# A gated delta rule kernel: the products of the state ahead of the coupling products, and the loads of the triangular solve shared by two DMA queues

## The chip, the cores and the metric

The kernel runs on one core of a Trainium2 chip. The metric is the device time of one launch in microseconds (us), from three runs. The engines are PE (matrix products), DVE and ACT (vector work), POOL (here memsets and DMA issues) and SP (DMA issues only). SP and POOL each own a DMA queue; both queues feed the same 16 DMA engines.

## The reference, cut to what matters

One layer for 2048 prompt tokens and 8 x 8 sample tokens. Half of it is windowed attention in three head groups with different strides; the other half, to which most of the change belongs, is the gated delta rule on 6 heads of width 128:

```python
lower = jnp.where(strict, jnp.einsum('...ik,...jk->...ij', kb, kc) * dmask, 0.0)
...
sol = lax.linalg.triangular_solve(jnp.eye(C) + lower, rhs, left_side=True, lower=True)
...
def step(S, xs):
    v_new = u_i - w_i @ S
    o = (q_i * jnp.exp(G_i)[..., None]) @ S + a_i @ v_new
    S = S * jnp.exp(g_last) + (k_i * jnp.exp(g_last - G_i)).T @ v_new
```

Every step needs the state S of the step before. The triangular systems do not depend on S.

## The kernel before, in words

The program is a row of blocks with a barrier between them: modulate, project (to about 1600 us of the trace), attend_prompt (to about 1800), attend_samples, delta_prompt (about 1862 to 2246), delta_samples and the tail with the output projections. The change is in attend_prompt and delta_prompt.

**delta_prompt** handles 16 chunks of 128 tokens in 8 pairs p. It is a software pipeline over the iteration `it` from -2 to 7: `grams` and `mask` build the systems of pair it+2 (tile UA), `solve` inverts the 32 x 32 diagonal blocks of a pair, `couple32`, `close32`, `couple64` and `close64` join these blocks into the inverse of the whole chunk (tile TT), and `of_state`, `solved` and `outputs` step the state S through chunks c = 2 it and c+1. The order on each engine is the order of the calls in the loop over ITS; engines meet at semaphores only.

The solve of all 96 blocks of a pair (2 chunks x 6 heads x 4 blocks) is one elimination on DVE, 31 pivots of two instructions in eight pieces. A block lies in it in one partition, which no engine can lay out, so the data goes through DRAM: `system(p)` on SP stores UA to u_d, waits for the store (u_out), and reads the diagonal blocks into sub_u with 8 DMAs of 384 runs of 128 bytes; `solution(p)` stores the result sub_w to w_d, waits (sub_out), and reads it into the diagonal of TT with 8 DMAs of 192 runs of 128 bytes. On DVE `turn_diag` waits for TT and makes the transposed blocks T, which `couple32` reads on PE; `gates` prepares decays for the pair after, `residual`, `state` and `result` are the DVE's part of the state's step. The step of a chunk goes kS (of_state) on PE, `residual` (rv) on DVE, Tr (solved) on PE, `new_values` (vn) on ACT, kv (outputs) on PE, `state` (S) on DVE. POOL issues only the store of each chunk's result (`store`).

In iteration `it` DVE runs residual(c), pieces 3 and 4 of the solve of pair it+1, state(c), pieces 5 to 7, mask(a), result(c), mask(a+1), residual(c+1), gates, turn_diag of pair it+1, state(c+1), pieces 0 and 1 of the solve of pair it+2, result(c+1), piece 2.

**attend_prompt** handles 3 groups of 16 blocks. DVE copies each block's result into the tile rows, SP stores it. The tile is one for all groups, so DVE waits at the start of groups 1 and 2 (`enter`) until the rows of the group before are stored. At the start of group 2 SP also begins the loads for attend_samples into space that groups 0 and 1 have left: five small ones, then the key cache kc in 8 parts. POOL scales q_s into q_bd_s when the five small ones are in.

## Time and profile before

| | us |
|---|---|
| median of 3 runs | 2910.11 |
| lowest, highest | 2894.85, 2912.45 |
| the profiled execution | 2896.57 |
| its span | 2894.9 |
| busy in the span: PE, DVE, ACT, POOL | 2608.3, 1083.4, 776.8, 153.3 |
| mean granted TensorE clock | 0.936 |

The profiled execution is one more run, with the time of the fast end of the three. The span is counted from the first to the last instruction; 1.7 us lie around it. Times of rows are microseconds from the start of the span.

### The profile page before, as it was taken

The numbers are of one execution on the slowest core, as the hardware profiler recorded it, in microseconds if no ns is written. First come the engines' busy times: TensorE is split into PE (matmuls) and PEld (weight loads), VectorE is DVE, ScalarE is ACT, GpSimd is POOL, SyncE is SP. The second block draws the span as 40 slices with busy tenths as digits, with TensorE's granted clock in tenths as the row PEclk, the third lists the DMA queues.
The fourth block names the chain that finished last, engine by engine and source line by source line (L and its number), as shares of the span: only waits on it lengthen the run. The fifth ranks groups of instructions, "written<-read, shape, count | busy, mean of one in ns | idle before, by whom it ended". The sixth has DMA issues, their size and how long they took to land. (4 is left out here: it accounts for less than half of the span.)

```text
span 2894.9 us, 41003 instructions
## 1 busy us (share of the span) xinstructions
PE 2608.3 (90%) x16430; PEld 2384.2 (82%) x16430; DVE 1083.4 (37%) x2593; ACT 776.8 (27%) x1677; POOL 153.3 (5%) x289
## 2 busy tenths in 40 slices
PE   6799999999999999999999798658777749999997
PEld 1799999999999999999999677347767539999775
DVE  3344444300000000000021465357775557675554
ACT  2222222211111111111100455234444123232343
POOL 0000000000000000000011000000000001111000
PEclk9899999999999999999999899768888669999998
DMA  7111112221111121111121715666443065555442
GB/s 282 61 70 69 69 69 77 82 75 67 67 67 67 67 83 72 67 67 67 68 79 46 303 36 201 210 140 159 111 107 109 29 216 162 179 177 191 146 141 75
DMA packets 249382, 320.42 MB, mean 111 GB/s; under 512 B 69874, under 2 KB 202242, under 8 KB 237348
## 3 DMA queue, kind: packets, MB, share of 16 engines
q1 hardware_dynamic: 201732, 201.46, 22.3%
q0 software_dynamic: 21136, 104.24, 9.5%
q10 hardware_dynamic: 26384, 12.98, 1.7%
q8 instruction: 82, 1.34, 0.2%
q14 instruction: 48, 0.39, 0.0%
HBM read 206.52 MB, written 112.11 MB: 110 GB/s over the span
## 5 line engine op out<-in xcount | busy, mean ns | idle before, releaser
L71 PE MATMUL ps_proj<-h_lo,w_hi 128*128 128x424 f32 (+1 forms) x2320 | 820.9, 354 | 26.1 <-DVE w_lo L401 26.1
L72 PE MATMUL ps_proj<-h_hi,w_lo 128*128 128x424 f32 (+1 forms) x2320 | 821.4, 354 | 0.0
L73 PE MATMUL ps_proj<-h_hi,w_hi 128*128 128x424 f32 (+1 forms) x2320 | 820.8, 354 | 0.0
L401 DVE TENSOR_TENSOR w_lo<-w_raw,w_hi 128x1024 fp32r<-128x1024 f32 x58 | 71.1, 1225 | 1080.7 <-ACT w_hi L320 1080.7
L71 PEld LDWEIGHTS ps_proj<-h_lo,w_hi 128*128 128x128 f32 x2320 | 436.3, 188 | 45.1 <-DVE w_lo L401 27.0
L72 PEld LDWEIGHTS ps_proj<-h_hi,w_lo 128*128 128x128 f32 x2320 | 436.0, 188 | 9.7
L73 PEld LDWEIGHTS ps_proj<-h_hi,w_hi 128*128 128x128 f32 x2320 | 436.1, 188 | 8.8
L358 ACT ACTIVATE stage<-ps_proj 128x424 f32<-128x424 f32 (+1 forms) x200 | 104.6, 524 | 755.8 <-PE ps_proj L73 755.8
L71 PE MATMUL ps_fm<-u_lo,w_tail_hi 128*128 128x256 f32 (+1 forms) x768 | 221.4, 288 | 11.6 <-DVE u_lo L2293 7.0
L72 PE MATMUL ps_fm<-u_hi,w_tail_lo 128*128 128x256 f32 (+1 forms) x768 | 219.6, 286 | 0.0
L73 PE MATMUL ps_fm<-u_hi,w_tail_hi 128*128 128x256 f32 (+1 forms) x768 | 219.4, 286 | 0.0
L71 PEld LDWEIGHTS ps_fm<-u_lo,w_tail_hi 128*128 128x128 f32 x768 | 146.2, 190 | 12.9 <-DVE u_lo L2293 7.6
L73 PEld LDWEIGHTS ps_fm<-u_hi,w_tail_hi 128*128 128x128 f32 x768 | 146.3, 190 | 0.0
L72 PEld LDWEIGHTS ps_fm<-u_hi,w_tail_lo 128*128 128x128 f32 x768 | 146.3, 190 | 0.0
L442 DVE SCALAR_TENSOR_TENSOR conv<-stage,side,conv 128x2048 f32<-128x2048 f32 x54 | 126.2, 2336 | 0.0
L71 PE MATMUL ps_out<-w_tail_lo,m_hi 128*128 128x512 f32 (+1 forms) x272 | 108.3, 398 | 0.3
L72 PE MATMUL ps_out<-w_tail_hi,m_lo 128*128 128x512 f32 (+1 forms) x272 | 107.5, 395 | 0.0
L73 PE MATMUL ps_out<-w_tail_hi,m_hi 128*128 128x512 f32 (+1 forms) x272 | 107.5, 395 | 0.0
L833 ACT ACTIVATE probs<-scores,neg 128x256 f32<-128x256 f32 (+1 forms) x192 | 86.2, 450 | 72.3 <-DVE neg L798 72.3
L368 ACT ACTIVATE conv<-conv 128x2112 f32<-128x2112 f32 x18 | 35.5, 1971 | 170.1 <-DVE conv L445 170.1
L1597 DVE TENSOR_TENSOR sub_prod<-sub_u,sub_w 96x126 f32<-96x126 f32 (+22 forms) x248 | 62.2, 251 | 42.8 <-DMA sub_u<-scratch_u_d 35.2
L1423 PE MATMUL ps_a<-xkq_first 128*128 128x256 f32 x96 | 31.2, 493 | 45.5 <-DVE UA L1584 32.0
(372 smaller groups left out, 3580.2 us busy)
## 6 DMA issues: line engine op xcount, KB each, us to landing
w_raw<-in_w_feat SPq DMA_DIRECT2D x58, 512.0 KB, 4.4
scratch_conv_d<-conv POOLq DMA_DIRECT2D x18, 1056.0 KB, 4.7
scratch_g_d<-stage POOLq DMA_DIRECT2D x16, 1056.0 KB, 4.5
gates<-scratch_g_d SPq DMA_DIRECT2D x56, 256.0 KB, 3.0
scratch_z_d<-stage POOLq DMA_DIRECT2D x12, 1056.0 KB, 4.5
ada_w<-in_w_ada SPq DMA_DIRECT2D x6, 2048.0 KB, 10.0
z_f<-scratch_z_d ACTq DMA_DIRECT2D x16, 768.0 KB, 5.0
kc<-in_k_cache SPq DMA_DIRECT2D x8, 1152.0 KB, 21.5
```

The lines of the kernel that those rows point to most:

```text
L71: pe.matmul(out, ah, bl, start=start, stop=False)
L72: pe.matmul(out, al, bh, start=False, stop=False)
L73: return pe.matmul(out, ah, bh, start=False, stop=stop)
L358: last = act.activation(stage[:, j, at:at + n], ps[:, c, 0:n], func)
L368: act.activation(conv[:, j, :], conv[:, j, :], ACT.Silu).then_inc(conv_silu, 1)
L401: dve.tensor_tensor(w_lo[:, j, 0:KT * P], w_raw[:, j, 0:KT * P], f32(w_hi[:, j, 0:KT * P]), ALU.subtract).then_inc(lo_done[j], 1)
L442: dve.scalar_tensor_tensor(out=conv[:, j, 0:SEQ], in0=stage[:, j, n:n + SEQ], scalar=w, in1=conv[:, j, 0:SEQ], op0=ALU.mult, op1=ALU.add). ...
L833: act.activation(probs[:, x.slot, p, h, 0:P * x.kb], scores[:, x.slot, p, h, 0:P * x.kb], ACT.Exp, bias=neg[:, x.slot, head:head + 1], acc ...
L1423: last = pe.matmul(A[bank_of(c, u)][:, 256 * (h % 2):256 * (h % 2 + 1)], x[:, h, 0, :], x[:, h, :, :].rearrange("p a n -> p (a n)"), start ...
L1597: dve.tensor_tensor(sub_prod[:, 0:n, 0:m], u[:, i:i + 1, i + 1:].broadcast_to([NSUB, n, m]), w[:, 0:n, i:i + 1].broadcast_to([NSUB, n, m]) ...
```

## The change

In delta_prompt the 8 loads of each system and of each solution are split: 4 are issued by SP as before, the other 4 by POOL, each half with a semaphore of its own, and DVE waits for both. On PE, `solved(c+1)` comes ahead of `couple32(b)` and `outputs(c+1)` ahead of `close32(b)`; on ACT, `new_values(c+1)` comes ahead of `keep32(b)`; on DVE, both `gates` come behind `state(c+1)`. In attend_prompt the rows of group 1 get a second home, the first part of the value tile of group 0, so that DVE waits only once, in group 2 for the rows of group 0. The key cache's last part lies over this home, so SP waits for the rows of group 1 before it, and the small loads (but for ident) come behind it.

```diff
@@ attend_prompt @@
-        rows = sb("rows", [P, NBLK, GW])
+        own_rows = sb("rows", [P, NBLK, GW])
+        rows = [own_rows, first["v"][:, 0], own_rows]
...
@@ SP, enter(g) for g == 2 @@
+                kc = lambda s: sp.dma_start(late["kc"][:, s], t["k_cache"][s]).then_inc(late["k_in"][s // HALF], 16)
                 sp.wait_ge(o_full, 2 * NBLK)
+                for s in range(NSEQ - 1):
+                    kc(s)
+                sp.dma_start(late["ident"][:, :], t["ident"]).then_inc(late["small_in"], 16)
+                sp.wait_ge(row_stored[1], 16 * NBLK)
+                kc(NSEQ - 1)
                 sp.dma_start(late["q_in"][:, :, :], t["q_d"][:, :, SEQ:].rearrange("a p n -> p a n")).then_inc(late["small_in"], 16)
...
-                sp.dma_start(late["ident"][:, :], t["ident"]).then_inc(late["small_in"], 16)
-                for s in range(NSEQ):
-                    sp.dma_start(late["kc"][:, s], t["k_cache"][s]).then_inc(late["k_in"][s // HALF], 16)
@@ DVE, attend_prompt @@
             def enter(g):
-                if g:
-                    dve.wait_ge(row_stored[g - 1], 16 * NBLK)
+                if g == 2:
+                    dve.wait_ge(row_stored[0], 16 * NBLK)
@@ delta_prompt @@
-        u_out, sub_in = sem("u_out"), [sem(f"sub_in{j}") for j in range(2)]
-        sub_out, tt_in = sem("sub_out"), [sem(f"tt_in{j}") for j in range(2)]
+        u_out, sub_in = sem("u_out"), [[sem(f"sub_in{s}{j}") for j in range(2)] for s in range(2)]
+        sub_out, tt_in = sem("sub_out"), [[sem(f"tt_in{s}{j}") for j in range(2)] for s in range(2)]
...
+        def load_solution(q, p, s):
+
+            q.wait_ge(sub_out, 16 * (p + 1))
+            q.wait_ge(zeroed, 1)
+            if p >= 2:
+                q.wait_ge(Tr, 4 * (p - 2) + 4)
+            w = t["w_d"][p].rearrange("(s a n) (c r) -> s a c n r", s=2, a=P // SUB, r=SUB)
+            for a in range(P // SUB):
+                dst = TT[p % 2].rearrange("p c h r -> p (c h) r")
+                q.dma_start(dst[SUB * a + s:SUB * (a + 1):2, :, SUB * a:SUB * (a + 1)], w[s, a]).then_inc(tt_in[s][p % 2], 16)
+
+        def load_system(q, p, s):
+
+            q.wait_ge(u_out, 32 * (p + 1))
+            if p >= 2:
+                q.wait_ge(sub_step, 2 * PIVOTS * (p - 1))
+            u = t["u_d"][p].rearrange("(a j) c h (b i) -> a b (c h) j i", j=SUB, i=SUB)
+            for a in range(P // SUB):
+                at = (NSUB // 2) * s + 2 * NHB * a
+                q.dma_start(sub_u[p % 2][at:at + 2 * NHB], u[a, a]).then_inc(sub_in[s][p % 2], 16)
...
@@ SP, solution(p) and system(p) @@
-                for s in range(2):
-                    for a in range(P // SUB):
-                        dst = TT[p % 2].rearrange("p c h r -> p (c h) r")
-                        sp.dma_start(dst[SUB * a + s:SUB * (a + 1):2, :, SUB * a:SUB * (a + 1)], w[s, a]).then_inc(tt_in[p % 2], 16)
+                load_solution(sp, p, 0)
...
-                for s in range(2):
-                    for a in range(P // SUB):
-                        at = (NSUB // 2) * s + 2 * NHB * a
-                        sp.dma_start(sub_u[p % 2][at:at + 2 * NHB], u[a, a]).then_inc(sub_in[p % 2], 16)
+                load_system(sp, p, 0)
@@ POOL @@
             for it in ITS:
+                if has(it + 1):
+                    load_solution(pool, it + 1, 1)
                 if has(it):
                     store(2 * it)
+                if has(it + 2):
+                    load_system(pool, it + 2, 1)
+                if has(it):
                     store(2 * it + 1)
@@ PE @@
                     turn_keys(b + 1)
-                    couple32(b)
                 if has(it):
                     solved(c + 1)
                 if has(it + 1):
+                    couple32(b)
                     turn_values(b + 1)
-                    close32(b)
                 if has(it):
                     outputs(c + 1)
                 if has(it + 1):
+                    close32(b)
                     couple64(b), couple32(b + 1)
@@ DVE @@
-                if has(it + 3):
-                    gates(a + 2), gates(a + 3)
                 if has(it + 1):
                     turn_diag(b), turn_diag(b + 1)
                 if has(it):
                     state(c + 1)
+                if has(it + 3):
+                    gates(a + 2), gates(a + 3)
@@ ACT @@
                     keys(b + 1)
-                    keep32(b)
                 if has(it):
                     new_values(c + 1)
                 if has(it + 1):
+                    keep32(b)
                     values(b + 1)
```

What stands on DVE in an iteration, from `residual(c+1)` to `state(c+1)`, before and after (rv is residual's tile, ET that of gates, S the state):

```order
L1619 SCALAR_TENSOR_TENSOR rv<-ps_c0,coef,bv1 128x128 x3
L1619 SCALAR_TENSOR_TENSOR rv<-ps_c1,coef,bv1 128x128 x3
L1574 TENSOR_TENSOR ET0<-G_in0,causal_T 128x768
L1574 TENSOR_TENSOR ET1<-G_in1,causal_T 128x768
L1609 STREAM_TRANSPOSE T0<-TT1 32x6x32 x3
L1609 STREAM_TRANSPOSE T1<-TT1 32x6x32 x3
L1628 SCALAR_TENSOR_TENSOR S<-S,coef,ps_c0 128x128 x3
L1628 SCALAR_TENSOR_TENSOR S<-S,coef,ps_c1 128x128 x3
```

```order
L1636 SCALAR_TENSOR_TENSOR rv<-ps_c0,coef,bv1 128x128 x3
L1636 SCALAR_TENSOR_TENSOR rv<-ps_c1,coef,bv1 128x128 x3
L1626 STREAM_TRANSPOSE T0<-TT1 32x6x32 x3
L1626 STREAM_TRANSPOSE T1<-TT1 32x6x32 x3
L1645 SCALAR_TENSOR_TENSOR S<-S,coef,ps_c0 128x128 x3
L1645 SCALAR_TENSOR_TENSOR S<-S,coef,ps_c1 128x128 x3
L1589 TENSOR_TENSOR ET0<-G_in0,causal_T 128x768
L1589 TENSOR_TENSOR ET1<-G_in1,causal_T 128x768
```

The two gates moved behind the update of the state. The transposes, which wait for the solution's load, stay ahead of it.

On PE, behind the turned keys of chunk c+1 (L1439, after L1454). Tr is L1522 (after L1537), couple32 L1465 and L1466 (after L1480 and L1481), and the turned values L1447. Before, the last two of the twelve products of couple32 and what follows; after, the last keys and what follows:

```order
L1465 MATMUL ps_a0<-T0,UA2 32x32
L1466 MATMUL ps_a1<-T0,UA2 32x32
L1522 MATMUL ps_c0<-rv,TT0 128x128 x3
L1522 MATMUL ps_c1<-rv,TT0 128x128 x3
L1447 MATMUL ps_a2<-ident_d,xv3 128x128 x3
L1447 MATMUL ps_a3<-ident_d,xv3 128x128 x3
```

```order
L1454 MATMUL ps_a2<-ident_d,xkq_first 128x128 x3
L1454 MATMUL ps_a3<-ident_d,xkq_first 128x128 x3
L1537 MATMUL ps_c0<-rv,TT0 128x128 x3
L1537 MATMUL ps_c1<-rv,TT0 128x128 x3
L1480 MATMUL ps_a0<-T0,UA2 32x32
L1481 MATMUL ps_a1<-T0,UA2 32x32
```

Tr now comes ahead of the twelve small products, which read the transposed solution T0. In the same way kv moved ahead of close32, and on ACT the copies to vn ahead of those to Y32.

On SP, from the load of a solution to the next gates' load, before and after:

```order
L1346 DMA TT0<-scratch_w_d 16x12x32 x8
L1351 DMA scratch_u_d<-UA2 128x6x128
L1351 DMA scratch_u_d<-UA3 128x6x128
L1359 DMA sub_u1<-scratch_u_d 12x32x32 x8
L1328 DMA G_in0<-scratch_G_rows 128x768
```

```order
L1317 DMA TT0<-scratch_w_d 16x12x32 x4
L1368 DMA scratch_u_d<-UA2 128x6x128
L1368 DMA scratch_u_d<-UA3 128x6x128
L1327 DMA sub_u1<-scratch_u_d 12x32x32 x4
L1353 DMA G_in0<-scratch_G_rows 128x768
```

Both loads are halved. The other halves stand on POOL, between the stores, which were all that POOL had in this block (L1405 is the store, L1327 the system's load, L1317 the solution's), here after:

```order
L1405 DMA scratch_o_d<-o_d0 128x768
L1327 DMA sub_u0<-scratch_u_d 12x32x32 x4
L1405 DMA scratch_o_d<-o_d1 128x768
L1317 DMA TT0<-scratch_w_d 16x12x32 x4
L1405 DMA scratch_o_d<-o_d0 128x768
```

## Rows read from the trace of the kernel before

**Rows 1.** Busy time of one period, and of four: x, instructions; last columns clock, DMA share, GB/s
```profile
2121.20:2162.30 41.10, 32.18 (x336) 29.30 (x336) 31.22 (x105) 19.85 (x66) 1.08 (x2) 0.87 0.33 82
sum 166.10, PE 130.92 PEld 119.46 DVE 124.98 ACT 79.39 POOL 4.32; mean PE 32.73 PEld 29.87 DVE 31.25 ACT 19.85 POOL 1.08
```

**Rows 2.** Waits in 1880 to 2260 us: total us, times, longest us
```profile
DVE S L1628 <- PE ps_c L1529: 36.2, 10, 5.3
DVE sub_prod L1597 <- DMA sub_u<-scratch_u_d: 35.2, 8, 12.6
```

**Rows 3.** Timeline of SP: start us, duration us, line, DMA issues
```profile
1996.23 0.34 SPq L1337 DMA_DIRECT2D scratch_w_d<-sub_w  x1
1998.35 5.17 SPq L1346 DMA_DIRECT2D TT<-scratch_w_d  x8
2003.56 1.19 SPq L1351 DMA_DIRECT2D scratch_u_d<-UA  x2
2007.94 3.63 SPq L1359 DMA_DIRECT2D sub_u<-scratch_u_d  x8
2011.61 0.89 SPq L1328 DMA_DIRECT2D G_in<-scratch_G_rows  x2
```

**Rows 4.** Instructions by tile, sub_w: the store of the solution, ns min/median/max, first and last start
```profile
L1337 SPq DMA_DIRECT2D scratch_w_d<-sub_w x8: 320/338/343, 1912.5 to 2204.6; - x8
```

**Rows 5.** Timeline of DVE, same period, columns as in rows 3
```profile
2001.13 1.64 DVE L1619 SCALAR_TENSOR_TENSOR rv<-ps_c,coef,bv 128x128 f32<-128x128 f32 x6
2002.69 1.82 DVE L1574 TENSOR_TENSOR ET<-G_in,causal_T 128x768 f32<-128x768 f32 x2
2005.08 2.29 DVE L1609 STREAM_TRANSPOSE T<-TT 32x192 f32<-32x192 f32 x6 [0.57 <-DMA TT<-scratch_w_d]
2012.34 1.64 DVE L1628 SCALAR_TENSOR_TENSOR S<-S,coef,ps_c 128x128 f32<-128x128 f32 x6 [4.97 <-PE ps_c L1529]
2016.70 0.19 DVE L1597 TENSOR_TENSOR sub_prod<-sub_u,sub_w 96x31 f32<-96x31 f32 x1 [2.73 <-DMA sub_u<-scratch_u_d]
...
2024.03 1.63 DVE L1619 SCALAR_TENSOR_TENSOR rv<-ps_c,coef,bv 128x128 f32<-128x128 f32 x6
```

**Rows 6.** Timeline of PE, same period
```profile
2002.94 0.82 PE L1439 MATMUL ps_a<-ident_d,xkq 128*128 128x128 f32 x6
...
2006.76 2.91 PE L1522 MATMUL ps_c<-rv,TT 128*128 128x128 f32 x12
...
2011.37 1.60 PE L1529 MATMUL ps_c<-vn,k_dec 128*128 128x128 f32 x12
...
2020.57 2.93 PE L1507 MATMUL ps_c<-S,xkq 128*128 128x128 f32 x12
```

**Rows 7.** Timeline of ACT, same period
```profile
2003.98 1.69 ACT L1684 ACTIVATE k_dec<-ps_a,coef 128x128 f32<-128x128 f32 x6
...
2008.42 0.49 ACT L1746 ACTIVATE vn<-ps_c 128x384 f32<-128x384 f32 x1 [0.89 <-PE ps_c L1522]
```

**Rows 8.** Groups of instructions of POOL over the span: busy us, mean ns
```profile
L510 POOL DMA_DIRECT2D out_v_out<-v_rows x51 | 27.6, 542 | 121.2 <-DVE v_rows L425 117.6 <-issue 3.7
...
L493 POOL DMA_DIRECT2D scratch_norm_d<-norm_rows x12 | 6.0, 500 | 0.5
```

**Rows 9.** Timeline of SP, last system load
```profile
2174.67 4.21 SPq L1359 DMA_DIRECT2D sub_u<-scratch_u_d  x8
```

**Rows 10.** Timeline of DVE, the wait for that load, and the last for a solution
```profile
2181.41 0.19 DVE L1597 TENSOR_TENSOR sub_prod<-sub_u,sub_w 96x31 f32<-96x31 f32 x1 [0.81 <-DMA sub_u<-scratch_u_d]
...
2213.52 2.29 DVE L1609 STREAM_TRANSPOSE T<-TT 32x192 f32<-32x192 f32 x6 [6.44 <-DMA TT<-scratch_w_d]
```

**Rows 11.** Waits in 1650 to 1810 us, prompt attention
```profile
DVE probs_T L809 <- DMA scratch_att_d<-rows: 3.6, 2, 1.8
```

**Rows 12.** Timeline of POOL, prompt attention
```profile
1766.51 4.81 POOL L702 TENSOR_SCALAR q_bd_s<-q_s 64x64 f32<-64x64 f32 x12 [9.86 <-DMA ident_s<-in_ident]
```

**Rows 13.** DMA issues of the page: KB each, median us from issue to landing
```profile
kc<-in_k_cache SPq DMA_DIRECT2D x8, 1152.0 KB, 21.5
```

More of the change, by code:

```diff
@@ L656, in store @@
                     dst = att.rearrange("(m s) n -> m s n", s=16)[:, x.b:x.b + 1]
-                src = rows[:, x.b:x.b + 1, :]
+                src = rows[x.g][:, x.b:x.b + 1, :]
                 sp.dma_start(dst, src if x.g else src.rearrange("p a n -> p (a n)")).then_inc(row_stored[x.g], 16)
@@ L803, in results @@
                 dve.wait_ge(o_full, x.u + 1)
-                dve.tensor_copy(rows[:, x.b:x.b + 1, 0:GW], ps_o[:, :, :].rearrange("p h d -> p (h d)").unsqueeze(1)
+                dve.tensor_copy(rows[x.g][:, x.b:x.b + 1, 0:GW], ps_o[:, :, :].rearrange("p h d -> p (h d)").unsqueeze(1)
                                 ).then_inc(o_read, 1)
@@ L1351, in system @@
                     sp.dma_start(t["u_d"][p, :, c % 2], UA[c % 6][:, :, 0, :]).then_inc(u_out, 16)
-                sp.wait_ge(u_out, 32 * (p + 1))
-                if p >= 2:
-                    sp.wait_ge(sub_step, 2 * PIVOTS * (p - 1))
-                u = t["u_d"][p].rearrange("(a j) c h (b i) -> a b (c h) j i", j=SUB, i=SUB)
-                for s in range(2):
-                    for a in range(P // SUB):
-                        at = (NSUB // 2) * s + 2 * NHB * a
-                        sp.dma_start(sub_u[p % 2][at:at + 2 * NHB], u[a, a]).then_inc(sub_in[p % 2], 16)
+                load_system(sp, p, 0)
             def samples():
@@ L1589, in solve @@
                 if piece == 0:
-                    dve.wait_ge(sub_in[p % 2], 128 * (p // 2 + 1))
+                    for s in range(2):
+                        dve.wait_ge(sub_in[s][p % 2], 64 * (p // 2 + 1))
                     dve.wait_ge(sub_ready[p % 2], 16 * (p // 2 + 1))
@@ L1603, in turn_diag @@
                 x = TT[c // 2 % 2][:, c % 2]
-                dve.wait_ge(tt_in[c // 2 % 2], 128 * (c // 4 + 1))
+                for s in range(2):
+                    dve.wait_ge(tt_in[s][c // 2 % 2], 64 * (c // 4 + 1))
                 if c >= 2:
```

5 lines of the change are left out of this document (removed).

## The prediction

> **What bounds the kernel now.** I read the page first, then the waits of delta_prompt, then its timelines, engine by engine, over one period of the pipeline. No engine fills this block: over four periods DVE is busy 31.25 us of some 41.5, PE 32.73, ACT 19.85, and POOL 1.08 [rows 1]. So a chain of waits sets the period. The store of the solution marks it: its first and last start are 7 periods apart, 292.1 / 7 = 41.7 us each [rows 4]. The waits name three places on DVE: state for kv, 36.2 us in all, solve for its system, 35.2 us in 8 waits (12.6 the longest, before the first solve) [rows 2], and turn_diag for its solution.
>
> The timelines show the order of these waits in one period. I call E the moment at which SP stores the solution, 1996.23 [rows 3]. The solution's 8 loads start at E+2.1 and take 5.17 us to issue; SP then stores the next system (E+7.3), waits for this to land, starts the 8 loads of the system at E+11.7 and issues them for 3.63 us [rows 3]. DVE starts to transpose at E+8.85, after 0.57 us of waiting, updates the state at E+16.1 after 4.97 us, and begins the next solve at E+20.5 after 2.73 us more [rows 5]. From there DVE runs through to the next E almost without a gap. So the period is 20.5 us of chain from E to the system's landing, and 41.9 - 20.5 = 21.4 us of DVE work. What the change can shorten is the first part.
>
> **Part 1, the order of the engines.** Nothing is added or removed: as many products, copies and DVE instructions as before. Before, Tr stood behind couple32 and so behind the solution: it ran from E+10.5, and kv from E+15.1 [rows 6]. Now PE can run Tr when residual has given rv (E+4.9 to 6.5, [rows 5]) and the keys are turned, E+7.5 [rows 6], so until about E+9.1 if it takes the 1.60 us that kv takes (in this period, after PE's wait, it took 2.91 [rows 6]; then it is E+10.4, and all that follows up to 1 us later). ACT has the next word: its keys end at E+9.4 [rows 7], and the two copies to vn take 0.49 each [rows 7], to E+10.4. Before, these stood behind the copies to Y32 and came at E+12.2 [rows 7]. On PE couple32 and the turned values stand between; I give them 1.7 us, the time from the end of Tr to kv in the trace, which held the values and close32 (2009.67 to 2011.37, [rows 6]). They are through at E+10.8, kv is done at E+12.4 and its first half at E+11.7. So state(c+1) runs from about E+11.7 to 13.3 instead of E+16.1 to 17.8. The gates, 1.82 us [rows 5], lay beside the wait for the solution; they now lie behind the state, to E+15.1. That is a cover that goes and a new one that is found, since DVE waits for the system there in any case. By itself this part is worth nothing: before and after, DVE then stands until the system lands, which no moved instruction makes earlier. It makes room for part 2, which the old order would stop at E+17.8, the end of the state. Its own bound is E+15.1: solve cannot begin sooner.
>
> Behind close32, which now stands after the outputs, PE still has its chain with ACT to of_state, from E+18.2 (kv's start, its 1.60 and as much less 0.1 for Av) to E+24.3 before [rows 6]. Shifted to E+14.0, with 0.6 for close32, it ends at E+21. kS takes up to 2.93 us [rows 6], to E+24; residual comes 7.33 us after the start of solve [rows 5], at E+23 or later, and takes its first half first. That just fits; I put up to 0.5 us per period on it in the range, none in the sum. The gates' later end also delays SP's next load of G_in, which waits for them, and on SP behind it the keys, queries and values. All these are for pairs that come one period later, so nobody waits; and they no longer run beside the system's load, which they did before (G_in issued at E+15.4 [rows 3], the system landing at E+20.5).
>
> **Part 2, the loads over two queues.** SP issues 4 solution loads in half of 5.17, 2.6 us, done at E+4.7. The mask of the second chunk is done before residual, so at E+4.9 [rows 5], and the stores of the system can follow: first issue E+4.75, both done at about E+5.9 in place of E+8.5. From the first store's start to the loads passed 2007.94 - 2003.56 = 4.4 us [rows 3], so the system's loads start at E+9.1 in place of E+11.7. That is 2.6 us, and needs only SP's half.
>
> How long from the start of these loads to their landing? Rows give 8.76 us in this period (2007.94 to 2016.70, [rows 3, 5]) and 6.74 in the last, with nothing behind it on the queue (2174.67 to 2181.41, [rows 9, 10]). With the issue halved and the queue free behind it, I take 6.7: the shorter issue could make it less (down to 6.74 - 1.8 = 4.9), but 3072 runs of 128 bytes take their own time. So the system lands at E+15.8, and solve begins there, just after the gates' E+15.1. Before, it began at E+20.5 in this period and at E+19.1 in a short one (2162.3 to 2181.41, [rows 1, 10]); I take the middle, 19.8. The gain is 4.0 us a period, 28 us over 7.
>
> The solution lands some 2.3 us sooner (half of the issue, 2.6, less the start of a second queue). In a full period it meets residual, which ends at E+6.5, so 8.85 - 6.5 is the most that it can give, and it lies on the way to the state, which is worked out above. After the last solve DVE waits 6.44 us for it [rows 10], with nothing beside it: there the 2.3 count, and part 1 takes the state off this wait; I put 3 us on the tail. The first system, waited for 12.6 us [rows 2], may gain 1.
>
> **POOL's price** is what the trace does not show: no DMA of POOL has 192 or 384 runs. Its nearest rows are 0.54 us for 128 rows of 1 KB and 0.50 us for a single row of 1.7 KB [rows 8]. A slope between them would make a load of 384 runs 0.6 us; a price in proportion to the runs, 0.54 / 128 x 384 = 1.6 us. I take 0.6 to 1.0, since the rows hardly differ between 1 row and 128. Four loads are then issued in 2.4 to 4 us, beside SP's 1.8, inside the 6.7. With x us for one load the half of POOL lands near E + 9.1 + 4x + 2.5, the 2.5 being the time from the last issue's end to the landing in the last period, 6.74 - 4.21 [rows 9, 10]. It passes E+15.8 at x = 1.05, and E+19.8, where the gain is gone, at x = 2.05. In order on POOL, store(2 it) now waits behind a solution's load. Results have two tiles and a period between them, so this costs nothing while POOL has some 15 us of work.
>
> The Trainium skill ("Perfetto Trace Analysis", section "DMA Instruction — SWDGE (GPSIMD)") says that the profiler's end of such a DMA is when the last DSP has generated its descriptors. By that, the 0.54 us holds the whole generation for 128 rows, which speaks for the low end of x; no run yet shows it for 384.
>
> **Part 3, attention.** DVE's waits for stored rows, 3.6 us in 2 [rows 11], go; PE and DVE hand work to each other there, so I count 3 of them. The small loads now come behind the key cache. POOL scaled q_s from 1766.5 to 1771.3 [rows 12], waited for by nobody before the block ends, at about 1800. A part of the key cache lands 21.5 us after its issue [rows 13], so the small loads may come some 22 us later than they did, and POOL's scaling ends at about 1793. It costs nothing, with 7 us to spare.
>
> **The sum:** 28 + 1 + 3 + 3 = 35 us less: 2896.57 - 35 = 2862 against the profiled execution, 2910.11 - 35 = 2875 against the median. The four times shown lie in two groups 15 us apart; I take their mean, 2903.5, and predict **2868 us**.
>
> **Rivals.**
> (a) The transfer, not the issue, sets the landing: halving gives nothing, and it stays 8.4 us from start to landing. Then the system lands at E+17.5, 2.3 a period, 16 over 7, and 22 in all: 2881. For it: 3.63 us of issue lie inside 8.76 to landing [rows 3, 5]. Against it: the 6.74 of the last load. The Trainium skill ("DMA: Bandwidth & Descriptors", section "Issuing engines are not separate DMA queues") holds with it: all DMAs run on the same 16 engines, and a second issuing engine only saves issue time, usually small beside the DMA. Here, by the rows, it is 3.63 of 8.76.
> (b) Everything goes as well as the order allows, solve starts at E+15.1 or a little before: 4.7 to 5 a period, 35, and 44 in all: 2859.
> (c) POOL generates by the run, 1.2 to 2 us for 384. At the 1.6 us in proportion its half lands at E+18.0, 1.8 a period, 13, and 19 in all with the other terms: 2885, and up to 2898.
> (d) **Slower:** POOL needs 3 us or more for 384 runs. DVE then waits for POOL's half alone. At 3 us it lands at E + 9.1 + 12 + 2.5 = 23.6, 3.8 a period later than now: +27, less 3 of attention: 2927. At 4 us it is +52. It decides from x = 2.05 us on; for it speaks only that no row shows such a DMA.
> (e) PE's chain after the outputs comes late for residual by 2 us a period: gain 2 a period, 21 in all: 2883.
>
> **Chances:** forecast 0.40, (a) 0.17, (b) 0.12, (c) 0.11, (d) 0.13, (e) 0.07. The range for 8 in 10 takes in (b) with the fast group of times, 2895 - 45 = 2850, and (a), (c) and (e) with the slow one: 2848 to 2912; it leaves (d) out. One per cent, 29 us, is about what a measurement of this kernel can tell from no change. Faster by over 1% (under 2881): most of the forecast, (b) and half of (a), 0.55. Slower by over 1% (above 2939): (d) with x above 3.2 us, 0.12. Within 1%: 0.33.
>
> **What the profile after would show.** Part 1: state's wait for kv under 1.5 us in a period, no wait of PE for T ahead of Tr. Part 2: the stores of the system at E+4.8, its loads at E+9.1, solve at E+15.8, periods of 37.7; DMA instructions of POOL under 1 us. Part 3: no wait of DVE in group 1 or 2. Wrong would be: DMA spans of POOL above 2 us, solve later than E+19, or a new wait of residual for kS.

## The result, and the profile after

| | before | after |
|---|---|---|
| median, us | 2911.11 (12 runs, 2891.71 to 2918.56) | 2887.93 (12 runs, 2885.82 to 2892.43) |
| ratio after / before | | 0.9928, 95% interval 0.991 to 0.9946 |
| profiled execution, span | 2896.57, 2894.9 | 2887.8, 2885.8 |
| clock of the profiled execution | 0.936 | 0.936 |

The change takes 23 us off the median, 0.7%, where the forecast was 2868, 43 less. The two profiled executions differ by only 9 us, and this difference between 23 and 9 is the first thing to explain. The stretches of the two traces, cut at the same instructions, add up as follows (us; E is, as in the prediction, the moment at which SP stores a solution, and a period runs from one E to the next).

| stretch | before | after | forecast of the difference |
|---|---|---|---|
| up to the first load of gates of delta_prompt | 1862.6 | 1858.2 (-4.4) | -3 |
| to the first store of a solution | 50.0 | 52.8 (+2.8) | -1 |
| 7 periods | 292.1 | 282.5 (-9.6) | -28 |
| to the store of the state | 40.1 | 36.7 (-3.4) | -3 |
| delta_samples | 87.1 | 89.3 (+2.2) | 0 |
| the rest | 563.1 | 566.3 (+3.2) | 0 |

**The periods.** First one row and the sum of four periods, in the view of busy times by stretch, columns as in [rows 1]:

```profile
2031.90:2071.43 39.53, 32.56 (x336) 29.94 (x336) 31.18 (x105) 19.79 (x66) 6.04 (x10) 0.86 0.62 146
...
sum 162.22, PE 135.36 PEld 124.41 DVE 124.74 ACT 79.68 POOL 24.13; mean PE 33.84 PEld 31.10 DVE 31.18 ACT 19.92 POOL 6.03
```

DVE has the same 31 us of work as in [rows 1] and PE 33.8 against 32.7; the rest of the difference is idle time. The waits of the block (total us, times, longest), which answer to [rows 2]:

```profile
DVE sub_prod L1613 <- issue: 26.9, 5, 9.6
DVE sub_prod L1613 <- DMA sub_u<-scratch_u_d: 22.0, 3, 15.6
...
DVE S L1645 <- PE ps_c L1544: 19.8, 9, 2.9
```

State's wait for kv fell from 36.2 to 19.8 us. In the period below 2.40 us of it are left, where the prediction had under 1.5, since DVE too comes to it sooner. Solve's wait for its system did not fall, it rose: 26.9 + 22.0 = 48.9 us against 35.2. In five of the eight it stands under "issue", for which the view names no releaser; DVE now waits there for two semaphores, one for each half.

One period in detail, E at 1991.95, SP first, then POOL, then DVE; they answer to [rows 3] and [rows 5]:

```profile
1991.95 0.34 SPq L1362 DMA_DIRECT2D scratch_w_d<-sub_w  x1
1994.07 2.52 SPq L1317 DMA_DIRECT2D TT<-scratch_w_d  x4
1996.63 1.18 SPq L1368 DMA_DIRECT2D scratch_u_d<-UA  x2
2001.93 1.74 SPq L1327 DMA_DIRECT2D sub_u<-scratch_u_d  x4
2005.65 1.64 SPq L1353 DMA_DIRECT2D G_in<-scratch_G_rows  x2
```

```profile
1994.33 2.19 POOL L1317 DMA_DIRECT2D TT<-scratch_w_d  x4 [18.17 <-DMA scratch_w_d<-sub_w]
...
2002.19 2.69 POOL L1327 DMA_DIRECT2D sub_u<-scratch_u_d  x4 [5.11 <-DMA scratch_u_d<-UA]
```

```profile
1998.43 2.29 DVE L1626 STREAM_TRANSPOSE T<-TT 32x192 f32<-32x192 f32 x6
2003.12 1.64 DVE L1645 SCALAR_TENSOR_TENSOR S<-S,coef,ps_c 128x128 f32<-128x128 f32 x6 [2.40 <-PE ps_c L1544]
2004.68 1.82 DVE L1589 TENSOR_TENSOR ET<-G_in,causal_T 128x768 f32<-128x768 f32 x2
2010.54 0.19 DVE L1613 TENSOR_TENSOR sub_prod<-sub_u,sub_w 96x31 f32<-96x31 f32 x1 [4.04 <-issue]
```

Read against E: SP's loads of the solution take 2.52 us to issue instead of 5.17, its stores of the system start at E+4.7 instead of E+7.3, the loads of the system at E+10.0 instead of E+11.7, with 5.3 us between store and load where there were 4.4 (why the stores take longer to land is not shown). DVE updates the state at E+11.2 instead of E+16.1, adds the gates behind it until E+14.6, and is then ready for the system. It begins the solve at E+18.6. From the start of its loads the system took 8.6 us, though only 1.74 us were spent on issuing on SP and 2.69 on POOL. PE and ACT went as worked out, in rows that answer to [rows 6] and [rows 7]: Tr done at E+8.9 (forecast 9.1), the copies to vn at E+10.2 (10.4), kv at E+11.8 (12.4).

```profile
1999.34 1.50 PE L1537 MATMUL ps_c<-rv,TT 128*128 128x128 f32 x12
...
2002.25 1.50 PE L1544 MATMUL ps_c<-vn,k_dec 128*128 128x128 f32 x12
```

```profile
2001.23 0.96 ACT L1763 ACTIVATE vn<-ps_c 128x384 f32<-128x384 f32 x2
```

The period before the last shows what else the second queue does. SP, POOL and DVE with E at 2111.67:

```profile
2121.71 1.74 SPq L1327 DMA_DIRECT2D sub_u<-scratch_u_d  x4
2123.49 0.43 SPq L1358 DMA_DIRECT2D sub_w<-in_sub_ident  x1
2123.97 1.01 SPq L1347 DMA_DIRECT2D xv<-scratch_conv_d  x2
```

```profile
2121.98 2.69 POOL L1327 DMA_DIRECT2D sub_u<-scratch_u_d  x4 [5.08 <-DMA scratch_u_d<-UA]
```

```profile
2132.81 0.19 DVE L1613 TENSOR_TENSOR sub_prod<-sub_u,sub_w 96x31 f32<-96x31 f32 x1 [6.71 <-issue]
```

The loads begin at E+10.0 again, but solve only at E+21.1, after 11.1 us. Here SP has no gates to wait for and issues its next loads right behind its 4. The trace's records of the semaphores have SP's half landed at 2129.2 and POOL's at 2132.7; in the period above it was 2009.4 and 2010.5. Over these 11.1 us the view of stretches has the DMA engines in use all the time (a share of 1.01), with 125 GB/s. The first period is the same: 10.9 us, solve at E+21.0. So is the first system of all, ahead of the first period: SP issues the next gates 1.78 us after the start of its half, and the system lands after 10.7 us where it took 7.4 before. This is the +2.8 of the second stretch.

And the last period, with nothing behind the system on either queue, answers to [rows 9] and [rows 10]:

```profile
2164.28 1.74 SPq L1327 DMA_DIRECT2D sub_u<-scratch_u_d  x4
```

```profile
2171.86 0.19 DVE L1613 TENSOR_TENSOR sub_prod<-sub_u,sub_w 96x31 f32<-96x31 f32 x1 [4.09 <-DMA sub_u<-scratch_u_d]
```

7.6 us from start to solve, with 4 loads on each queue; before, it was 6.7 with 8 on one, and 7.1 to 7.2 in two other kernels of the table below that have 8 on one. POOL's own DMAs are cheap, by the view of groups, against [rows 8]:

```profile
L1327 POOL DMA_DIRECT2D sub_u<-scratch_u_d x32 | 21.6, 680 | 58.3 <-DMA scratch_u_d<-UA 57.6 <-issue 0.7
L1317 POOL DMA_DIRECT2D TT<-scratch_w_d x32 | 17.5, 554 | 167.3 <-DMA scratch_w_d<-sub_w 167.3
```

384 runs cost 0.68 us and 192 runs 0.55. A run here is a contiguous piece of the load's pattern. The trace does not list POOL's runs one by one: the page counts 69874 packets under 512 bytes before and 51698 after, 18176 fewer, about as many as the 18432 runs that moved to POOL.

Means over the 7 periods, from the same kind of rows in the kernels on which the argument rests (the experiments follow):

| kernel | period | solve begins | from the start of the system's loads | in each of the 7 periods |
|---|---|---|---|---|
| before | 41.7 | E+19.8 | 7.9 | 7.7, 7.0, 8.8, 8.1, 8.7, 8.0, 6.7 |
| after | 40.4 | E+19.0 | 9.0 | 10.9, 7.7, 8.6, 8.0, 8.9, 11.1, 7.6 |
| the wait put back, else as after | 40.4 | E+19.0 | 8.8 | 10.5, 8.7, 8.6, 7.4, 8.4, 11.0, 7.2 |
| order and attention, no second queue | 41.7 | E+20.2 | 8.0 | 7.8, 9.4, 8.7, 6.8, 8.2, 8.1, 7.2 |
| two queues alone | 41.7 | E+20.4 | 10.0 | 10.4, 8.6, 11.5, 10.7, 11.0, 10.3, 7.6 |
| system on SP | 39.2 | E+17.5 | 7.4 | 7.3, 6.9, 8.1, 6.9, 8.1, 7.5, 7.1 |
| SP holds | 39.7 | E+18.2 | 7.8 | 7.3, 7.5, 8.1, 7.5, 7.9, 9.0, 7.4 |
| half the system | 38.9 | E+15.3 | 5.1 | 4.4, 5.9, 5.0, 4.8, 5.4, 5.7, 4.4 |
| compact | 38.9 | E+14.9 | 4.2 | 3.6, 4.2, 4.3, 3.5, 4.4, 5.8, 3.6 |
| compact, kS sooner | 37.0 | E+15.4 | 4.1 | 3.6, 3.6, 5.3, 4.7, 3.5, 4.4, 3.6 |

The third row has the same delta_prompt as the second and repeats it, the two late landings too. In the last three DVE is often not ready before the system is, so their last columns are upper bounds.

### The profile page after: what moved, and what is told of

The parts are those of the page before. It is cut to its first block and busy times, and to the rows that moved or that the text cites. A ratio compares the mean times of both kernels' runs of the same rounds, so it can differ in the third digit from the quotient of the medians.

```text
span 2885.8 us, 41026 instructions
## 1 busy us (share of the span) xinstructions
PE 2605.5 (90%) x16430; PEld 2381.5 (83%) x16430; DVE 1082.9 (38%) x2593; ACT 777.0 (27%) x1677; POOL 192.8 (7%) x353
## 2 busy tenths in 40 slices
DMA packets 232101, 320.43 MB, mean 111 GB/s; under 512 B 51698, under 2 KB 184578, under 8 KB 220068
## 3 DMA queue, kind: packets, MB, share of 16 engines
q0 software_dynamic: 23184, 106.62, 10.1%
## 5 line engine op out<-in xcount | busy, mean ns | idle before, releaser
L71 PEld LDWEIGHTS ps_proj<-h_lo,w_hi 128*128 128x128 f32 x2320 | 436.3, 188 | 45.0 <-DVE w_lo L401 26.9
L1613 DVE TENSOR_TENSOR sub_prod<-sub_u,sub_w 96x126 f32<-96x126 f32 (+22 forms) x248 | 62.1, 250 | 56.5 <-issue 26.9
L1438 PE MATMUL ps_a<-xkq_first 128*128 128x256 f32 x96 | 30.2, 478 | 49.3 <-DVE UA L1599 36.2
## 6 DMA issues: line engine op xcount, KB each, us to landing
ada_w<-in_w_ada SPq DMA_DIRECT2D x6, 2048.0 KB, 10.3
```

Source lines behind the costliest of these rows:

```text
L71: pe.matmul(out, ah, bl, start=start, stop=False)
L1438: last = pe.matmul(A[bank_of(c, u)][:, 256 * (h % 2):256 * (h % 2 + 1)], x[:, h, 0, :], x[:, h, :, :].rearrange("p a n -> p (a n)"), start ...
L1613: dve.tensor_tensor(sub_prod[:, 0:n, 0:m], u[:, i:i + 1, i + 1:].broadcast_to([NSUB, n, m]), w[:, 0:n, i:i + 1].broadcast_to([NSUB, n, m]) ...
```

## The experiments

Two theories stood at the start. The one of the prediction: issuing sets when a system lands, so half of the issue is worth 2 us a period. The other: the runs take the DMA engines' time whoever issues them, and the second queue gives up the order that one queue kept. That the profiles differ by 9 us and the medians by 23 pointed to a third thing outside the block.

### The parts alone

Each is the kernel before with one part of the diff.

> Before, with the new order of PE, ACT and DVE in delta_prompt alone: all loads on SP, attention as before. Theory T (the landing of the system's load sets the start of solve, and no moved instruction makes it earlier): the state goes forward to about E+12 to 13, solve stays at E+19 to 20.5, the period at 41.7, 0 us (within 3) against before. Rival O (the order by itself is what gave the block its gain, because keys, values and states of the next pair hang on it): periods of some 40.4, 8 to 10 us less than before.

Measured: 2907.4 us, ratio 0.9973 (0.9949 to 0.9997). Periods of 41.2, the state at E+12 to 13, solve at E+19.9. 5 of its 12 executions lie in the faster of two groups of times that the next section explains, against 14 of 76 of the kernel before; within either group it is some 2 us faster. So the order alone is worth next to nothing, as both this expectation and the prediction had it.

> Before, with the two queues alone: the order of the engines and attention as before. Theory T: the loads of the system start at about E+10 instead of E+11.7 and land 7 to 8.5 us later; the solution lands some 1.5 us sooner and with it the state, which ends at about E+16.5, so it hardly stops solve: periods of 40 to 40.8, 7 to 12 us less than before, nearly all that the changed kernel gained in this block. As the prediction had it (the old order stops solve at the end of the state, E+17.8, after a landing at E+15.8): 2.0 us a period, 14 less. Rival O: 0 to 2 us less.

Measured: 2916.94 us, ratio 1.0003 (0.9989 to 1.0018). **The expectation missed:** no gain at all, periods of 41.7. Within either group of times it is even 4 to 6 us slower than before; its trace has some 5 us more behind the block. The system's loads begin at E+10 here too, but land 10.0 us later in the mean. The old order is the likely reason, and the runs of the section on the landing bear it out. It adds the gates before the solution is turned, so SP's wait for them is over, and SP issues the next gates, keys and queries right behind its half of the system. One period, E at 2009.19, SP, POOL and DVE:

```profile
2019.15 1.74 SPq L1323 DMA_DIRECT2D sub_u<-scratch_u_d  x4
2020.93 0.90 SPq L1349 DMA_DIRECT2D G_in<-scratch_G_rows  x2
```

```profile
2019.42 2.69 POOL L1323 DMA_DIRECT2D sub_u<-scratch_u_d  x4 [5.10 <-DMA scratch_u_d<-UA]
```

```profile
2030.64 0.19 DVE L1609 TENSOR_TENSOR sub_prod<-sub_u,sub_w 96x31 f32<-96x31 f32 x1 [5.10 <-issue]
```

From 2019.15 to 2030.64 are 11.5 us. In the changed kernel the gates stand behind the state and SP's next load comes 3.7 us after its half of the system instead of 1.8. So the two queues need the new order, and one reason is not to be seen in the diff: the new order holds SP's other loads back.

> Before, with the attention part alone (second home for the rows of group 1, small loads behind the key cache). As predicted: 3 us less, delta_prompt begins 3 to 4.5 us earlier and the rest keeps its length. Rival: the gain is lost by the end of the block or given back behind it, 0 us.

Measured: 2892.49 us, ratio 0.9934 (0.9921 to 0.9947). A part to which the forecast gave 3 us gives 20, nearly all of the change's gain by the median. **This expectation missed too.** delta_prompt begins 4.9 us earlier than in the profile of before, and its periods stay at 41.7.

### Where 20 us come from: the clock

The executions of the kernel before lie in two groups, 2891 to 2901 and 2904 to 2919. Where the clock of each is known, the first group has a mean granted clock of 0.933 to 0.938 and the second one of 0.923 to 0.928, with no exception in 64 executions. Of all 76, 14 are in the first group, and the profile of before that the prediction was read from is one of them. The profile of the variant with the order alone is of the second. It and the changed kernel, by stretches of 10 us, the column before the last two being the granted clock:

```profile
1750.00:1760.00 10.00, 8.73 (x64) 7.94 (x63) 4.42 (x29) 5.25 (x24) 1.37 (x1) 0.89 0.39 99
1760.00:1770.00 10.00, 10.00 (x54) 8.34 (x53) 5.44 (x39) 4.87 (x23) 3.44 (x10) 0.50 1.00 407
1800.00:1810.00 10.00, 10.00 (x54) 8.67 (x54) 5.23 (x40) 4.59 (x20) 0.00 (x0) 0.50 0.11 39
```

```profile
1750.00:1760.00 10.00, 10.00 (x79) 8.71 (x79) 6.66 (x44) 5.58 (x26) 1.37 (x1) 1.00 0.48 166
1760.00:1770.00 10.00, 10.00 (x78) 8.54 (x77) 7.15 (x55) 7.30 (x35) 0.00 (x0) 1.00 1.02 425
```

Between 1750 and 1760 PE is busy for 8.73 us and idle for 1.27: this is DVE's wait for the stored rows at the start of group 2. In the first kernel the granted clock then falls to 0.50, 1.2 GHz instead of 2.4, and stays there while PE is busy all the time, 54 products in 10 us instead of 78, to the end of attend_prompt. In the second PE has no such gap and keeps 1.00 until it runs out of work, after 1790. In the profile of before the gap was there (8.74 us busy in the same stretch) and the clock held. delta_prompt begins at 1878.8 in the first kernel, at 1862.6 in the profile of before.

To separate the wait from the rest of the attention part, it was put back alone:

```diff
             def enter(g):
                 if g == 2:
-                    dve.wait_ge(row_stored[0], 16 * NBLK)
+                    dve.wait_ge(row_stored[1], 16 * NBLK)
```

> The changed kernel, with one wait put back in prompt attention: DVE waits for the stored rows of group 1 before it writes those of group 2, though these now have a tile of their own. Theory C (the gain of the attention part lies mostly in the clock: PE stands idle for 1.3 us in this wait, around 1755, and in most executions its granted clock then falls to 0.50 for some 60 us, to the end of the block): most executions are back 15 us above the others, median 2903 to 2908, profile with a clock of 0.50 from 1760 on. Rival W (the wait costs its own 1.8 us and no more): 2889 to 2891.

Measured: 2908.57 us, ratio 0.9991 (0.9967 to 1.0016); 10 of 12 executions at 2904 to 2913 with a clock of 0.922 to 0.927, two at 2887 and 2891 with 0.933 and 0.934. The wait costs 1.8 us where it stands, and the profile shows what follows:

```profile
DVE probs_T L813 <- DMA scratch_att_d<-v_first: 1.8, 1, 1.8
```

```profile
1750.00:1760.00 10.00, 8.82 (x71) 7.82 (x69) 4.94 (x37) 4.74 (x21) 1.37 (x1) 0.97 0.25 72
1760.00:1770.00 10.00, 10.00 (x51) 8.65 (x51) 5.20 (x36) 5.61 (x26) 0.00 (x0) 0.50 1.00 412
1800.00:1810.00 10.00, 10.00 (x54) 8.56 (x55) 4.91 (x30) 5.78 (x27) 0.00 (x0) 0.50 0.09 30
```

So it is this wait that brings the fall of the clock, not always but in 10 of 12 executions, and a wait of 1.8 us costs about 20. The other half of the attention part, the later small loads, was tried on the kernel before:

```diff
                 sp.wait_ge(o_full, 2 * NBLK)
+                for s in range(NSEQ):
+                    sp.dma_start(late["kc"][:, s], t["k_cache"][s]).then_inc(late["k_in"][s // HALF], 16)
...
-                for s in range(NSEQ):
-                    sp.dma_start(late["kc"][:, s], t["k_cache"][s]).then_inc(late["k_in"][s // HALF], 16)
```

> Before, with the small loads behind the key cache and nothing else; the rows of the three groups share one tile and DVE waits for their stores as before. Theory C (only the wait makes PE idle and lets the clock fall): same two groups of times as before, most executions at 2906 to 2918, median within 3 us of before. Rival M (the small loads, issued ahead of the key cache, disturb group 2): 2895 or less in all executions.

Measured: 2908.45 us, ratio 0.9985 (0.9961 to 1.0008), again in two groups, 2896 to 2901 and 2904 to 2916. By itself it takes neither the wait nor the two groups away. The Trainium skill ("TensorE: Matmul & The Clock Gate", section "Part 1: The HAM clock gate") says that the gate watches PE's activity in a window that runs free of the kernel, so that one kernel can come out differently from run to run. The two groups of one and the same kernel fit that, though no run here shows the window. That the low clock outlasts the gap by 50 us of a busy PE does not follow from it; the rows above show it.

### The landing of the system

```diff
             def system(p):
...
                 load_system(sp, p, 0)
+                load_system(sp, p, 1)
@@ POOL @@
-                if has(it + 2):
-                    load_system(pool, it + 2, 1)
```

> The changed kernel, with all 8 loads of the system on SP again; the solution stays on two queues, the order stays new. Theory T (3072 runs of 128 bytes take some 7 us of the DMA engines whichever queue they come from, and on one queue nothing that SP issues later can pass them): landing 6.7 to 8.7 us after the start of the loads, solve at E+17 to 18.7, also in the first period and the one before the last, where it now comes at E+21: 3 to 10 us less than the changed kernel. Rival I (issue sets the landing, as the prediction took it): 8 issues take 3.6 us instead of 1.8, landing 1.8 us later in each period, 7 to 13 us more than the changed kernel.

Measured: 2875.95 us, ratio 0.9872 (0.9856 to 0.9888), 12 us less than the changed kernel, somewhat more than theory T had. The period before the last, E at 2104.90, SP and DVE:

```profile
2114.88 3.64 SPq L1327 DMA_DIRECT2D sub_u<-scratch_u_d  x8
2118.56 0.41 SPq L1358 DMA_DIRECT2D sub_w<-in_sub_ident  x1
```

```profile
2122.34 0.19 DVE L1612 TENSOR_TENSOR sub_prod<-sub_u,sub_w 96x31 f32<-96x31 f32 x1 [1.44 <-issue]
```

Twice the issue on SP, 3.64 us, and SP's other loads right behind it as in the changed kernel; yet the system is there after 7.5 us instead of 11.1. The prediction's theory of issue gave 7 to 13 us more for this kernel. It is out. A second change kept the halved issue and took away only what SP issues behind it:

```diff
                 load_system(sp, p, 0)
+                sp.wait_ge(sub_in[1][p % 2], 64 * (p // 2 + 1))
```

> The changed kernel, with one wait more on SP: after its own 4 loads of a system SP waits until the half of POOL has landed, and issues nothing before. Theory Q (in the first period and the one before the last POOL's half comes 4 us late because SP's next loads, of gates, identities and values, share the DMA engines with it): solve at E+17.5 in these two periods as well instead of E+21, POOL's half landing within 8 us of its start everywhere; 5 to 8 us less than the changed kernel. Rival P (POOL's half is late by itself, by its descriptors): E+21 stays, and the time is the same or above.

Measured: 2877.85 us, ratio 0.9891 (0.9854 to 0.9928), 10 us less than the changed kernel, where 5 to 8 were expected. Solve begins at E+18.3 and E+18.9 in the two periods, not at E+17.5. The same period, E at 2106.82:

```profile
2116.78 1.74 SPq L1327 DMA_DIRECT2D sub_u<-scratch_u_d  x4
2125.69 0.33 SPq L1358 DMA_DIRECT2D sub_w<-in_sub_ident  x1
```

```profile
2125.75 0.19 DVE L1614 TENSOR_TENSOR sub_prod<-sub_u,sub_w 96x31 f32<-96x31 f32 x1 [2.94 <-issue]
```

POOL's half comes within 9.0 us here and within 7.3 in the first period, where it took 11.1 and 10.9. So most of its delay came from what SP issued next, not from itself; 9.0 is still more than the 8 us expected, and what the rest is stays open. The Trainium skill ("DMA: Bandwidth & Descriptors", section "Queues, rings and completion order") says that each DMA engine takes turns between the queues that have work for it. The times of these two kernels agree with that: on one queue the gates and values stand behind the system, from two queues they share the engines with POOL's half. The turns themselves no row shows. The mean from start to landing is still 7.8 us, with half of the issue and nothing in its way, no less than the 7.9 of the kernel before.

> The changed kernel without POOL's half of the system's load: the second 48 partitions of the system stay zero, so half of the solutions are wrong, and 1536 runs of 128 bytes are loaded in place of 3072. Theory T (the runs take the DMA engines' time): landing some 5 us after the start, solve at E+14.5 to 15.5, bound by the gates, periods of 37 to 38. Rival L (a fixed latency of the load sets its landing): solve stays at E+17 to 17.7, periods above 39.

Measured, in a single run: 2871.05 us, span 2869.2. Half of the runs land in 5.1 us in the mean, 4.4 at best, against 7.8 for all of them without interference. Since POOL's issue is gone here too, these 2.7 us could in part be issue. SP's own half settles it: its 4 loads are issued in 1.7 us in both kernels, and by the semaphores' records they land 6.9 us after their start in the mean where SP holds and 4.9 here. So POOL's half costs SP's half 2.0 us though SP issues the same in both; this is transfer and not issue. The last period, in which nothing else is loaded, says the same in GB/s (the last number) and in the share of the DMA engines' time (before it); here the kernel before, the changed kernel, and half the system, each from the first to the last of the system's packets:

```profile
2175.60:2180.80 5.20, 5.20 (x68) 4.77 (x66) 1.64 (x6) 2.95 (x10) 0.00 (x0) 0.82 0.59 77
```

```profile
2165.20:2170.30 5.10, 4.28 (x72) 4.05 (x71) 1.64 (x6) 3.27 (x11) 2.04 (x4) 1.00 0.94 79
```

```profile
2148.10:2150.50 2.40, 2.40 (x33) 2.28 (x33) 1.64 (x6) 1.35 (x6) 0.00 (x0) 1.00 0.53 82
```

One queue or two, all or half, the system comes at some 80 GB/s. The second queue made the engines busier, 0.94 of the time instead of 0.59, but moved the 384 KB no faster. What holds the rate at 80 is not shown.

But solve at E+15.3 gave periods of 38.9, not 37 to 38; the wait that took over is below.

```diff
-    sp.dma_start(t["u_d"][p, :, c % 2], UA[c % 6][:, :, 0, :]).then_inc(u_out, 16)
+    own = t["u_d"][p].rearrange("a c h j i -> c a j h i")
+    for a in range(P // SUB):
+        r = slice(SUB * a, SUB * (a + 1))
+        sp.dma_start(own[c % 2, a], UA[c % 6][r, :, 0, r]).then_inc(u_out, 16)
...
-    for a in range(P // SUB):
-        at = (NSUB // 2) * s + 2 * NHB * a
-        q.dma_start(sub_u[p % 2][at:at + 2 * NHB], u[a, a]).then_inc(sub_in[s][p % 2], 16)
+    at = (NSUB // 2) * s
+    q.dma_start(sub_u[p % 2][at:at + NSUB // 2].rearrange("p j i -> p (j i)"), u).then_inc(sub_in[s][p % 2], 16)
```

> The variant with the whole system on SP, where the store of the system writes only the diagonal blocks, in the order of the systems (8 DMAs of 192 runs of 128 bytes instead of 2 of 768 runs of 512), so that the load is 2 DMAs of 48 runs of 4 KB instead of 8 of 384 runs of 128 bytes. Theory T (the count of runs sets the landing): stores issued by E+8.5, landed by E+10.5, loads landed within 3 us, solve at about E+14 to 15, bound by the gates; periods of 36.5 to 38, 10 to 18 us less than the variant with the whole system on SP. Rival S (the scattered stores take as long as the loads did): solve at E+17 or later, no gain over that variant.

Measured: 2871.31 us, ratio 0.9868 (0.983 to 0.9906). The first period, E at 1907.00, where DVE waits for it:

```profile
1912.76 3.99 SPq L1370 DMA_DIRECT2D scratch_u_d<-UA  x8
1917.94 0.78 SPq L1326 DMA_DIRECT2D sub_u<-scratch_u_d  x2
```

```profile
1921.55 0.19 DVE L1614 TENSOR_TENSOR sub_prod<-sub_u,sub_w 96x31 f32<-96x31 f32 x1 [2.99 <-DMA sub_u<-scratch_u_d]
```

The same 384 KB to the same 96 partitions land in 3.6 us when they are 96 runs of 4 KB, where 3072 runs of 128 bytes took 7.3 in this period (system on SP). In the last period they come at 196 GB/s:

```profile
2153.40:2155.30 1.90, 1.13 (x40) 0.90 (x38) 0.03 (x1) 0.96 (x3) 0.00 (x0) 1.00 0.72 196
```

So it is not the bytes. The edit cuts the runs from 3072 to 96 and at the same time the loads from 8 to 2 and their issue from 3.6 us to 0.8; how much each of these gives was not tried apart. The store has 8 issues, 3.99 us, and 5.2 us lie between its start and the load, no more than in the changed kernel. Solve could begin at E+14.5, where the gates end; but the period is 38.9, 0.9 us above the range expected, and the gain over the variant with the system on SP is 5 us instead of 10 to 18, with 4 executions of each whose times overlap. **The expectation was too high.**

What took over is in the waits of DVE in 1910 to 2180, half the system first, then compact:

```profile
DVE rv L1636 <- PE ps_c L1523: 16.6, 19, 3.3
```

```profile
DVE rv L1637 <- PE ps_c L1523: 19.3, 19, 2.8
```

Residual waits 2.4 to 2.8 us in a period for kS. This is rival (e) of the prediction, which appears only when solve begins early enough. The last kernel moves the products for it:

```diff
                     close64(b), close32(b + 1)
+                    keys_of_state(b)
                     couple64(b + 1)
                     close64(b + 1)
...
                 if has(it):
-                    of_state(c)
+                    queries_of_state(c)
```

> The variant with the compact system, with one move more on PE: the products of the keys with the state (kS) of the next pair stand between close32(b + 1) and couple64(b + 1), not behind close64(b + 1). Theory F (with solve at E+14.5 the chain of PE and ACT to kS is what sets the period, 38.9 us: DVE's residual waits some 3 us for it): the wait of rv goes, periods of 36 to 37.5, 8 to 18 us less than the compact variant, 2853 to 2863. Rival K (the moved products only push back the chain of T, which Tr of the next pair needs): no gain, 2869 to 2874.

Measured: 2856.67 us, ratio 0.9812 (0.9774 to 0.9851), periods of 37.0, all as theory F had it, and the wait is nearly gone:

```profile
DVE rv L1641 <- PE ps_c L1523: 1.9, 5, 0.6
```

### The changed kernel without its second queue

This kernel has the new order and the attention part, with all loads on SP.

> The changed kernel without its second queue: new order and attention as changed, all 8 loads of the solution and all 8 of the system on SP, as before. Theory T (the order alone gives 0.4 us a period, as in the variant with the order alone; the solution's half on POOL gives 2 us a period by letting SP's chain start 1.7 us sooner; the system's half on POOL takes 1.1 us a period back): periods of 41.2, 2887 to 2890, as much as the changed kernel within 2 us and 12 to 14 above the variant with the whole system on SP. POOL's DRAIN at the end of delta_prompt is back at 1.4 us, and the blocks behind it at 87 and 563 us. Rival O (the order is what gained): 2878 to 2882.

Measured: 2889.85 us, ratio 0.9925 (0.9899 to 0.9952), and the two stretches behind the block at 87.3 and 563.0 us, as expected. The periods are 41.7, not 41.2; the profiled execution is one of the two longest of its 6, 2894.47 us. Rival O is out. The medians, of 4 to 12 executions each (76 for before), then give a chain of steps: before 2912; attention 2892.5 (-20); the order 2889.9 (-3, not resolved); the solution on two queues, the system on SP 2876.0 (-14); the system's half to POOL 2887.9 (+12). The change as made is the first three gains and this loss.

## Why the prediction was wrong

The forecast was 2868, the sum 35 us from 2903.5. Measured are 23 us from 2911. It is wrong in its largest term, and a small one was wrong the other way: the periods gave 9.6 us and not 28, attention 20 by the median and not 3. That the gain came within 12 us of the forecast is luck, made by two errors of opposite sign.

**The step that failed:** "With the issue halved and the queue free behind it, I take 6.7" from the start of the system's loads to their landing. It took 9.0 in the mean, 7.6 to 11.1. Two things are in it. The 6.74 of the last period before was taken as the landing with the queue free, and the 2 us above it in another period as what the longer issue and the loads behind it had cost. But 6.74 already was the time of 3072 runs issued over 4.21 us; with the issue halved the last period took 7.58, and 7.4 where SP holds. Halving the issue saved nothing. And "the queue free behind it" is false for POOL's half: behind SP's half come SP's other loads, and they share the engines with it. The mean of before was 7.9, so the split made the landing 1.1 us later. That takes back more than half of the 1.9 us that the loads start sooner in the mean (E+10.1 against E+12.0).

- **SP's chain:** the stores at E+4.75 came at E+4.7. The system's loads came at E+10.0, not E+9.1: their wait for the stores is 5.3 us and not 4.4, for a reason that is not shown. A miss of 0.9 a period, 6 us over 7, within the same term.
- **Part 1:** right. State at E+11.2 (forecast 11.7), gates to E+14.6 (15.1), worth next to nothing by itself (periods of 41.2 with the order alone, 41.7 without a second queue). Its link with part 2 was seen only as room for solve. That it also holds back SP's gates was noted ("they no longer run beside the system's load"), but priced as if one queue kept its order.
- **The floor of kS:** "That just fits" was wrong by 1.2 us. With half the system solve began at E+15.3, sooner than the forecast E+15.8, and the period was 38.9, not 37.7. So even a landing as forecast would have been worth about 2.8 us a period, 20 and not 28; moving kS forward took the period to 37.0.
- **POOL's price:** right, 0.68 us for 384 runs, taken as 0.6 to 1.0. Rivals (c) and (d) fall with it. What was missed is POOL's DRAIN at the end of the block (below).
- **The first system:** forecast -1, measured +2.8; POOL's half of it too shared the engines with SP's next loads, and it landed after 10.7 us instead of 7.4.
- **The tail:** -3 forecast, -3.4 measured.
- **Attention:** "I count 3 of them" was right for the wait and wrong for the time. -4.4 between the profiles, -20 between the medians, since the clock no longer falls. The prediction saw "two groups 15 us apart" and took the mean of the four times as its base; what made the groups was not asked, and the profile at hand, from the first group, could not show it; only the list of times did.
- **Rival (a)** had the right mechanism in its first half: transfer and not issue. Its 2881 left out the other queue and the clock. The 2885 of (c) lay nearer, for a reason that did not hold. The sentence beside it from the Trainium skill ("DMA: Bandwidth & Descriptors", section "Issuing engines are not separate DMA queues"), that a second issuing engine saves only issue time, agrees with the runs: SP's issue fell from 3.6 to 1.7 us, and no landing came sooner.
- **Sums:** those of three rivals are a microsecond or two off: the terms of (a) make 23 and not 22, of (b) 42 and not 44, of (c) 20 and not 19. No range or chance hangs on it.

With the terms as measured: -4.4 + 2.8 - 9.6 - 3.4 + 2.2 + 3.2 = -9.2, the difference of the profiled spans (9.1); and some 14 more for the clock, in the median only.

## What to carry over

A second queue for one load is not half the time. The system came at some 80 GB/s over one queue or two, and the first queue's later loads shared the engines with the second queue's half. Splitting the solution paid (-14 us), since SP came to its next store sooner; splitting the system, which must land before the loads behind it, cost 12. Fewer loads of longer runs shortened the landing more than any split. Where a kernel's times lie in two groups, compare the granted clock of their stretches before anything else: a wait of under 2 us in a dense stretch of products made the slower group possible here. And when a wait is to be taken away, work out at what point the next one begins; here kS took over, and the period stopped 1.2 us above the forecast.

## What was not expected of the hardware

- After PE had been idle for 1.3 us in 10, the granted clock fell to 0.50 and stayed there for 50 us of a PE that was busy all the time; by the times and mean clocks this happened in 62 of 76 executions of the kernel before, and in 14 the clock held. The profiles of both kinds show the same gap.
- A block in which POOL issues loads of 192 or 384 runs ends later. The trace records POOL's DRAIN at the end of delta_prompt with 1.37 us in every kernel without such loads and with 3.65 (changed kernel) or 3.98 us with them. The next block waits for it; here is DVE's wait for the block's start in the variant with attention alone, then in the changed kernel:

```profile
DVE Y_e L1932 <- PEq L1264: 5.0, 1, 5.0
```

```profile
DVE Y_e L1945 <- PEq L1264: 7.3, 1, 7.3
```

  That is the 2.2 us of delta_samples in the table. Why POOL's DRAIN is longer no run shows. The last stretch is 2 to 4 us longer in seven of the eight kernels with POOL's loads, 565.4 to 566.8 against 562.9 to 563.4 (563.8 in the eighth, where SP holds); what causes this stays open.
- 3072 runs of 128 bytes on one queue took 6.7 to 9.4 us to land in the kernels of the table, 384 KB at some 80 GB/s; the same 384 KB in 96 runs of 4 KB landed in 3.6 us, at some 200.
